# Delta-rule stage of a two-layer trunk: sums of squares in two single-pass products, and a new order on four engines

## The reference

```
def gated_delta_chunked(q, k, v, g, beta):   # q, k: unit norm per head
    G = jnp.cumsum(g, axis=-1)
    decay = jnp.where(incl, jnp.exp(jnp.where(incl, diff, 0.0)), 0.0)
    kk = jnp.einsum('bhnid,bhnjd->bhnij', k, k)
    lower = jnp.eye(CHUNK) + jnp.where(strict, beta * decay * kk, 0.0)
    sol = lax.linalg.triangular_solve(lower, rhs, ...)
    ...
    def step(S, inp):                         # over the chunks
        u = u_b - w_c @ S
        o = qd @ S + a_c @ u
        S = S * exp(gl) + kd.T @ u
...
q = l2_normalize(heads(qkv[..., :GDN_WIDTH]))          # x * rsqrt(sum(x*x) + EPS)
k = l2_normalize(heads(qkv[..., GDN_WIDTH:2 * GDN_WIDTH]))
```

## Time and profile before

| | |
|---|---|
| median of 3 runs | 3044.75 us (3042.94 to 3045.47) |
| the profiled execution | 3046.14 us, its span 3044.4 us |
| PE busy | 2972.9 us, 98% |
| DVE, ACT, POOL busy | 1531.4, 851.8, 426.4 us |
| mean granted TensorE clock | 0.99 of full speed |

### The profile page before, as it was taken

One profiled execution on the slowest core, in us unless ns is written; L12 is line 12 of the kernel. 1 busy time (PEld: TensorE's weight loads), 2 busy tenths in 40 slices (PEclk: granted clock), 3 DMA queues, 4 the chain that ended last, 5 costly groups with the idle time before them and its releaser, 6 DMA issues.

```text
span 3044.4 us, 47051 instructions
## 1 busy us (share of the span) xinstructions
PE 2972.9 (98%) x19124; PEld 2689.6 (88%) x19124; DVE 1531.4 (50%) x2163; ACT 851.8 (28%) x1521; POOL 426.4 (14%) x503
## 2 busy tenths in 40 slices
PE   8999989999999999999999999999999999999998
PEld 7999978887899999999999998788888888888887
DVE  5777447776443343444346443666743433333444
ACT  4211235555221111111113101566612111111112
POOL 2000145554120000000000000000021000100000
PEclk9999989999899999999999999999999999999999
DMA  3333321211111111111111425545211111111111
GB/s 121 92 92 98 107 72 52 63 63 57 33 57 49 41 48 48 41 41 48 49 48 38 151 86 165 140 99 118 59 49 56 41 55 48 48 44 46 48 41 70
DMA packets 201815, 207.31 MB, mean 68 GB/s; under 512 B 8363, under 2 KB 172348, under 8 KB 201676
## 3 DMA queue, kind: packets, MB, share of 16 engines
q1 hardware_dynamic: 191098, 167.05, 18.9%
q0 software_dynamic: 10368, 38.21, 3.7%
q10 hardware_dynamic: 210, 0.07, 0.0%
HBM read 162.87 MB, written 42.44 MB: 67 GB/s over the span
## 4 chain that ended last, share of the span: by engine, by line
PE 93%; DVE 2%; ACT 2%; issue 2%; POOL 1%; ACTq 0%; DVEq 0%; POOLq 0%
PE PS L1824 20%; PE PS L1823 20%; PE PS L1822 20%; PE PS L2237 5%; PE PS L2236 5%; PE PS L2235 5%; PE PS L2358 2%; PE PS L2342 2%; PE PS L2034 1%; PE PS L2309 1%; PE PS L2014 1%; PE PS L2308 1%; PE PS L1961 1%; DVE dec L1404 1%; PE PS L2051 1%
## 5 line engine op out<-in xcount | busy, mean ns | idle before, releaser
L1822 PE MATMUL PS<-YH,WL 128*128 128x348 f32 (+1 forms) x3040 | 1039.6, 342 | 4.4 <-DVE WL L1254 3.0
L1823 PE MATMUL PS<-YL,WH 128*128 128x348 f32 (+1 forms) x3040 | 1039.2, 342 | 0.0
L1824 PE MATMUL PS<-YH,WH 128*128 128x348 f32 (+1 forms) x3040 | 1038.4, 342 | 0.0
L1822 PEld LDWEIGHTS PS<-YH,WL 128*128 128x128 f32 x3040 | 572.0, 188 | 45.3 <-DVE WL L1254 3.3
L1823 PEld LDWEIGHTS PS<-YL,WH 128*128 128x128 f32 x3040 | 571.6, 188 | 37.9 <-issue 0.8
L1824 PEld LDWEIGHTS PS<-YH,WH 128*128 128x128 f32 x3040 | 573.0, 188 | 35.6
L1647 DVE TENSOR_TENSOR hT<-PS,hT 128x346 f32<-128x346 f32 (+2 forms) x440 | 251.3, 585 | 178.7 <-PE PS L2237 178.7
L2235 PE MATMUL PS<-AH,WL 128*128 128x346 f32 (+2 forms) x880 | 308.6, 351 | 1.1 <-DVE AL L1637 1.1
L2237 PE MATMUL PS<-AH,WH 128*128 128x346 f32 (+2 forms) x880 | 308.8, 351 | 0.0
L2236 PE MATMUL PS<-AL,WH 128*128 128x346 f32 (+2 forms) x880 | 308.8, 351 | 0.0
L794 POOL TENSOR_TENSOR gact<-gact,rs 128x346 f32<-128x346 f32 (+2 forms) x110 | 118.8, 1080 | 1307.0 <-ACT gact L1096 1307.0
(11 more groups left out here) (282 smaller groups left out, 3729.2 us busy)
## 6 DMA issues: line engine op xcount, KB each, us to landing
raw<-in_ffn_w_gate_up SPq DMA_DIRECT2D x88, 512.0 KB, 3.7
raw<-in_ffn_w_down SPq DMA_DIRECT2D x44, 512.0 KB, 3.6
s_in<-obuf POOLq DMA_DIRECT2D x32, 520.0 KB, 4.4
raw<-in_gdn_w_in SPq DMA_DIRECT2D x32, 512.0 KB, 4.2
Xqk<-s_in SPq DMA_DIRECT2D x10, 832.0 KB, 4.5
raw<-in_w_kv SPq DMA_DIRECT2D x16, 512.0 KB, 3.9
Xv<-s_in SPq DMA_DIRECT2D x10, 416.0 KB, 3.2
gBc<-s_g SPq DMA_DIRECT2D x10, 416.0 KB, 3.5
```

The lines of the kernel that those rows point to most:

```text
L1822: pe.matmul(PS[:, bank, 0:n], wl, xh, start=(k == 0), stop=False)
L1823: pe.matmul(PS[:, bank, 0:n], wh, xl, start=False, stop=False)
L1824: m = pe.matmul(PS[:, bank, 0:n], wh, xh, start=False, stop=(k == KT - 1))
```

## The change

`squares_high` on ACT squares keys and queries into a float32r tile `sqh` (one buffer for both g). POOL still makes the full squares, and `squares_low` on POOL subtracts the high part, giving `sql`. `key_sums` adds two float32r products, ones times high and ones times low, in place of each float32 product; chunk 0 keeps the old form. SP waits for `squares_high` of chunk c-2 ahead of the `Xqk` load. The loops of PE, ACT, DVE and POOL are written in a new order.

```
+            def squares_low(h, g):
+                pool.wait_ge(cs["sq"][g], h + 1)
+                pool.wait_ge(cs["shi"][g], h)
+                pool.tensor_tensor(sql[g][:, :, :], sq[g][:, :, :], sqh[:, :, :].bitcast(F32), ALU.subtract).then_inc(cs["slo"][g], 1)
...
+            def squares_high(h, g):
+                act.wait_ge(c_load, 16 * (h + 1))
+                if g:
+                    act.wait_ge(cs["kn"][0], h + 1)
+                else:
+                    act.wait_ge(cs["kn"][1], h)
+                src = Xqk[:, :, :].rearrange("p (w h) j -> p w h j", w=2)[:, :, HG * g:HG * g + HG, :]
+                act.activation(sqh[:, :, :].rearrange("p w (h j) -> p w h j", h=HG), src, ACT.Square).then_inc(cs["shi"][g], 1)
...
 (SP, ahead of the Xqk load of step c)
+                    if c > 1:
+                        sp.wait_ge(cs["shi"][g], c - 1)
...
 (PE, key_sums)
+                pe.wait_ge(cs["slo"][g], h)
+                for w in range(2):
+                    pe.matmul(PS[:, b0 + w, 0:GW], onesr[:, :], sqh[:, w, :], start=True, stop=False)
+                    m = pe.matmul(PS[:, b0 + w, 0:GW], onesr[:, :], sql[g][:, w, :], start=False, stop=True)
+                m.then_inc(cs["ss"][g], 1)
```

More of the change, by code:

```diff
@@ L743, in _ @@
                 tail, head = 0 <= t, h < NC
+                if tail:
+                    mask(t, 5, 0)
                 if levels:
-                    decayed(c, 1, 0)
+                    decayed(c, 0, 1)
                 if tail:
                     mask(t, 6, 0)
[L748 to L753, removed]
+                    mask(t, 6, 1)
                 if head and h:
@@ L756, in _ @@
                 if levels:
+                    first_mask(c, 0)
+                    decayed(c, 1, 0)
+                    first_mask(c, 1)
+                if head and h:
+                    squares_low(h, 0)
+                if levels:
                     mask(c, 1, 1)
+                    mask(c, 1, 0)
                     mask(c, 2, 1)
[L759 to L762, removed]
+                    mask(c, 2, 0)
                 if head and h:
                     squares(h, 1)
+                if levels:
+                    mask(c, 3, 1)
+                    decayed(c, 1, 1)
+                    mask(c, 4, 1)
+                    mask(c, 3, 0)
+                    mask(c, 4, 0)
+                    mask(c, 5, 1)
+                if tail and t < NC - 1:
+                    fade(t, 0)
+                if head:
+                    decayed(h, 0, 0)
+                if head and h:
+                    squares_low(h, 1)
                 if tail and t < NC - 1:
                     fade(t, 1)
[L767 to L776, removed]
             def accumulate(ph):
@@ L1001, in _ @@
                 if levels:
+                    values(c, 0)
+                if head and h:
+                    squares_high(h, 0)
+                if levels:
                     values(c, 1)
-                if head:
-                    decays(h, 1)
-                if levels:
+                    copy_x(c, 0, 1)
                     copy_x(c, 0, 0)
-                    copy_x(c, 0, 1)
-                    later_half(1, 1)
+                    later_half(c, 1, 1)
+                    later_half(c, 1, 0)
                 if head and h:
@@ L1011, in _ @@
                 if levels:
-                    later_half(1, 0)
+                    copy_x(c, 1, 1)
+                    later_half(c, 2, 0)
+                    copy_x(c, 1, 0)
+                if tail:
+                    result(t, 0)
+                if levels:
+                    later_half(c, 2, 1)
                 if head:
@@ L1015, in _ @@
                 if levels:
-                    copy_x(c, 1, 1)
-                    later_half(2, 1)
+                    copy_x(c, 2, 1)
+                if head and h:
+                    squares_high(h, 1)
+                if levels:
+                    later_half(c, 3, 1)
                 if tail:
                     result(t, 1)
[L1020 to L1023, removed]
                 if c == NC - 1:
@@ L1027, in _ @@
                 if levels:
[L1028 to L1033, removed]
+                    later_half(c, 3, 0)
+                    copy_x(c, 2, 0)
+                    copy_x(c, 3, 1)
                 if head and h:
@@ L1046, in _ @@
                     result_norm(t, 0)
+                if levels:
+                    copy_x(c, 4, 1)
+                    copy_x(c, 4, 0)
+                if tail:
+                    result_norm(t, 1)
                 if c == NC - 1:
@@ L1519, in _ @@
                     unit(h, 0)
[L1520 to L1524, removed]
                 if levels:
@@ L1534, in _ @@
                     low(0, 1)
+                if levels:
+                    add_u(c, 3, 1)
                 if head and h:
@@ L1537, in _ @@
                 if levels:
-                    add_u(c, 3, 1)
                     add_u(c, 3, 0)
-                if head:
-                    keys(h, 0)
+                if tail and t < NC - 1:
+                    state(t, 1)
+                    state(t, 0)
                 if tail:
-                    gated(t, 1)
+                    gated(t, 0)
                 if levels:
@@ L1565, in _ @@
                     first_m(h, 1)
-            gated(NC - 1, 0)
+                    keys(h, 1)
+                if tail:
+                    gated(t, 1)
+                if levels:
+                    updates(c, 1)
+                if c == NC:
+                    lo(2, P_GO.job0 + 3)
+                    lo(3, P_GO.job0 + 4)
             low(2, 0)
@@ L1953, in key_products @@
                     pe.wait_ge(cs["rn"][1], 1)
+                if h == 0 and g == 1:
+                    pe.wait_ge(taken, TAKEN0[P_GO])
                 if h > 1 and g == 0:
@@ L2107, in _ @@
                 tail, head = 0 <= t, h < NC
+                if levels:
+                    turned(c, 1)
                 if tail:
                     solved(t, 1)
+                if levels:
+                    level_x(c, 0, 1)
+                    level_x(c, 0, 0)
+                if tail:
                     solved(t, 0)
@@ L2118, in _ @@
                 if levels:
-                    level_u(c, 0, 0)
-                    level_u(c, 0, 1)
+                    level_x(c, 1, 1)
+                    level_x(c, 1, 0)
+                if tail:
+                    outputs(t, 0)
+                if levels:
+                    level_u(c, 1, 1)
                 if tail:
                     outputs(t, 1)
+                if c == NC:
+                    go_chunk(*GO_ORDER[1])
                 if levels:
-                    level_x(c, 1, 1)
+                    level_u(c, 1, 0)
+                    level_x(c, 2, 1)
                 if tail and t < NC - 1:
@@ L2127, in _ @@
                 if levels:
[L2128 to L2135, removed]
+                    level_u(c, 2, 1)
+                    level_x(c, 2, 0)
+                    level_x(c, 3, 1)
                 if tail and t < NC - 1:
@@ L2140, in _ @@
                 if levels:
[L2141 to L2146, removed]
+                    level_u(c, 2, 0)
+                    level_u(c, 3, 1)
+                    level_x(c, 3, 0)
                 if c == NC:
@@ L2166, in _ @@
                     level_x(c, 4, 0)
-                if head:
-                    turned(h, 1)
+                if tail:
+                    output_sums(t, 1)
+                if c == NC:
+                    go_chunk(*GO_ORDER[3])
                 if levels:
@@ L2172, in _ @@
                 if head:
+                    key_products(h, 0)
                     key_products(h, 1)
                 if levels:
+                    level_x(c, 5, 1)
                     level_x(c, 5, 0)
-                    level_x(c, 5, 1)
+                if head:
+                    turned(h, 0)
+                if levels:
+                    level_u(c, 5, 1)
+                    from_state(c, 1)
+                    level_u(c, 5, 0)
                 if head:
```

72 lines of the change are left out of this document (27 added, 45 removed).

## The result

| | before | after |
|---|---|---|
| median | 3045.11 us (4 runs, 3042.94 to 3046.45) | 3096.29 us (4 runs, 3092.26 to 3106.48) |
| ratio | | 1.017 (95% interval 1.0156 to 1.0184) |
| profiled execution | 3046.14 us | 3092.26 us |
| DVE, ACT, POOL busy | 1531.4, 851.8, 426.4 us | 1547.6, 868.4, 460.8 us |
| mean granted clock | 0.990 | 0.985 |

The change makes the kernel 51 us slower; 3076 was forecast, with a range up to 3092. The sign and the large step of the mechanism (a late load that PE waits for) came as predicted. A second wait came out more than twice as long as summed, and with it the size.

The account below looks back on a forecast made before the run. PE's own work was taken as the bound. Rounds 1 to 7 lose 4.5 us each (31.5), round 8 wins 1.3, early rounds add 1: 3046.1 becomes 3077.3, median 3076; own range 3060 to 3092, 8-in-10 range 3033 to 3092.

Parts of the forecast that it names:

- The sign: Whole kernel: slower than before, 3076 us forecast; slower had a chance of 0.71, faster 0.20.
- large step: Ahead of `first_t(h, 0)`: PE idles 2.65 us a round, as POOL's `first_mask` stands behind `squares` and the late `Xqk` load.
- A second wait: PE at `level_x(c, 3, 0)`: waits for `add_u(c, 2, 0)`, held behind `differences(h, 0)` on DVE; 0.9 us a round.
- The second wait: PE behind `first_t(h, 0)`: waits another 0.7 us a round while POOL does `decayed` and `first_mask(h, 1)`.
- the small one: PE at `level_x(c, 3, 0)`: waits 0.9 us, bounds 0 to 1.5, for `add_u(c, 2, 0)` behind the moved `differences(h, 0)`.
- round 8: Round 8 of the delta stage: no further load, so it wins 1.3 us.
- The 2.5 us taken for a round: Behind the gaps at `first_t`: the clock falls each round, costing 1.6 to 3.4 us, taken as 2.5.
- the round of 36.5 us at full clock: Delta-stage round: 33.56 - 1.28 + 0.9 + 2.65 + 0.7 = 36.5 us, 2.0 more than before.
- The clock stays up: Rival: the gap ahead of `first_t` comes but the clock does not fall; 3059 us, chance 0.15.
- The new order holds: Rival: PE remains bound by its work and both gaps at `first_t` vanish; 3033 or 3025 us, chance 0.20.
- About even: Rival: landing after 4.6 us and `differences` in its short form, a round of 34.4; 3045 us, chance 0.08.
- Float32r no cheaper: Rival: float32r passes of `key_sums` cost as much as float32, 12 us more on top; 3088 us, chance 0.02.

Follow-up runs that it names:

- e7: Changed kernel plus three useless float32 products on PE ahead of the wait of `first_t(h, 0)` in rounds 1 to 7; 3097.17 us, ratio 1.0166.
- e3: Changed kernel, but SP issues the `Xqk` load ahead of the `gBc` load; 3062.78 us, ratio 1.0060 to the kernel before.
- e4: Changed kernel, but POOL does both `first_mask` and `decayed(c, 1, 0)` ahead of `squares(h, 0)`; 3070.53 us, ratio 1.0078 to the kernel before.
- e8: Changed kernel with `decays(h, 1)` on ACT moved to directly behind `norms(h, 1)`; 3064.28 us, ratio 1.0065 to the kernel before.
- e5: Changed kernel with `differences(h, 0)` on DVE moved behind `add_u(c, 3, 0)`; 3073.23 us, ratio 1.0092 to the kernel before.
- e2: Changed kernel with the float32 `key_sums`, without `squares_high`, `squares_low` and SP's wait (new order alone); 3076.96 us, ratio 1.0100 to the kernel before.
- e10: Changed kernel with `differences(h, 0)` later on DVE and three useless products ahead of `first_t(h, 0)` in rounds 1 to 7; 3067.13 us, ratio 1.0073.
- e9: Changed kernel with `Xqk` load first and `differences(h, 0)` later, but the old float32 products, without `squares_high` and `squares_low`; 3040.24 us, ratio 0.9986.
- e6: Changed kernel with both repairs, `Xqk` load ahead of `gBc` and `differences(h, 0)` behind `add_u(c, 3, 0)`; 3035.34 us, ratio 0.9964 to the kernel before.
- e1: Kernel before, in its old order, with only the new float32r products added; 3049.14 us, ratio 1.0013.

## Why the prediction was wrong, and where it was right

**The large step was right**, and its size too. From PE's start behind `output_sums(t, 1)` (689.83) to `first_t(h, 0)` (701.39) pass 11.56 us; 11.5 was summed. The gap was 2.06 to 2.99 us in rounds 1 to 7, 2.6 on average (2.65), the landing 5.8 us (5.8), `squares_low` 1.95 (2.05). The second wait, for `first_mask(h, 1)`, was 0.70 as computed where the clock was up (e7), and hidden where it was low. e3, e4 and e8 each take the gap away by a different link of the chain, which shows the chain.

**The step that failed is the small one: `level_x(c, 3, 0)`.** I bounded that wait by 0 and 1.5 us, the 1.5 from no row, and took 0.9, the size it had in its old place. It was 2.13 to 2.15 in every one of the eight steady rounds, 1.25 over the term, and e5, which takes it away, runs 23 us faster. The fault lies in taking L1404's 3.65 us as the long form although I had just put the longer `squares_low` beside it: each of the four instructions waits for about one POOL item, so 1.96 + 1.06 + 0.7 + 1.07 gives 4.8, against 4.83 measured. With 3.65 us the same chain would leave about 2.15 - 1.18 = 0.97 us, by my estimate, so the 0.9 was right for the length that it was read at. e2 (no `squares_low`: 2.19 us, no gap) and e5 show that cause. I had the mechanism in the lock that the Trainium skill describes (SBUF — State Buffer, "SBUF: two separate sides"), and the trace agrees with it (0.95 us alone, 4.83 beside POOL); I did not carry the new item's length through it.

**What hung on it.** First, a gap of 2.15 us is itself large enough to lower the clock, and the sum had one fall in a round. The trace after has falls behind both gaps, the second kind in four of eight rounds (at 520, 643, 684 and 766 us); one such fall costs 1.5 us in e3. Second, round 8, which I had winning 1.3 us because it has no late load, also has this gap with its fall, and it begins in the low stretch that round 7's late mask leaves behind: 38.90 us, 4.4 lost.

**Clock.** The 2.5 us taken for a round was too much, and a mistake on the other side hid part of that. A fall behind `first_t` costs about 0.9 net (e10), not 1.6 to 3.4; I had not asked who sets the pace just after the gap. The falls at the second gap, which I did not have, add 1.5 in about every second round, so that the two kinds together come to some 1.6 a round (an estimate from e3 and e10).

**Not seen at all:** `gated(t, 1)` at the round's end also runs beside `squares_low` and the masks (its two instructions take 1.94 and 1.84 us at 664.99, against 0.58 and 0.65 for `gated(t, 0)`) and delays `add_u`, so `level_x(c, 1, 1)` waits 0.34 to 0.87 us in five of the rounds 1 to 7 (0.46 on average); and PE's bare work in the new order is 34.0 us (e9) against 33.56 before, a term of 0.45, spread in pieces of some 0.1 us over many groups, for which I have no cause. `key_sums` went to 0.83, not 0.76. With these, the round of 36.5 us at full clock becomes 36.5 + 1.25 + 0.46 + 0.45 + 0.14 + 1.6 = 40.4, against 40.7 measured. My range had no place for this: the terms named with it, the dearest clock and 5 us for the ends, add up to 3087 and not to its 3092, and none stands for a second fall in a round.

Together, for the profiled execution: rounds 1 to 7 took 40.7 on average, 6.2 over 34.49, 43.5 us in all (31.5 forecast); round 8 +4.4 (-1.3); the rounds ahead +4.4, of them 2.1 until the first `first_t` (+1); the end from `first_t` of the last chunk to the output projection 42.8 against 48.5 us, -5.7 (0). The same stretch takes 43.9 to 44.2 us in e2, e3, e6 and e9 and 47.5 in e1, so its gain belongs to the new order; the mean granted clock in it is 0.75 before and 0.88 after, and no run tests more than that. The four parts add up to 46.6 us, against 46.1 measured. The median lies 4 us above that execution: the four runs span 14 us, and the longer the run, the lower its mean clock (0.985 at 3092.26, 0.983 at 3094.55, 0.982 at 3098.03, 0.979 at 3106.48). That fits a number of falls that differs from run to run; it was not tested by itself. Before, with gaps of 0.93 us, four runs span 3.5 us and the thirteen timed beside e1 6.2.

**The rivals.** "The clock stays up" (3059) fell by the windows. "The new order holds" (3033) describes the repaired kernel (3035), not this one; what separated the two were the late load and the late differences. "About even" (3045) fell by both of its conditions: the landing took 5.8 us and `differences` 4.83. "Float32r no cheaper" fell: 0.83 against 1.40.

## What to carry to other kernels

Where an order is written out by hand, follow each load back through the DMA queue to the last instruction it waits for, and price it issued as it will be, behind its neighbour: one `decays` moved by a third of a round turned a load with time to spare into a gap in every round. And when work is added to GpSimd, give every VectorE instruction beside it that reads two operands from SBUF the new item's length, not the length it showed before. Near 98% of TensorE, two such repairs (one DMA earlier, one DVE item later) were worth 61 us, and the cheaper products 5 to 7.

## What the runs showed of the hardware that was not expected

- Gaps of like length do not always lower the granted clock. In the changed kernel it fell behind the gap at `first_t` (2.06 to 2.99 us) in every one of rounds 1 to 7, but behind the 2.13 to 2.15 us at `level_x(c, 3, 0)` in four of eight; in e3 seven of eight steady rounds fell behind 2.14 us, and the one from 639.09 to 674.44 did not. A gap of 1.64 us in round 0 of the changed kernel (at 456.47) was followed by a fall, one of 1.54 at the same place in e5 was not. Most low stretches in the steady rounds lasted 3.4 us, a few 6.8.
- A fall of the clock costs less where another engine sets the pace behind it: 1.5 us in e3 (36.88 against 35.35), some 0.9 net behind `first_t` (e5 against e10, 3073.23 to 3067.13), where PE waits for POOL as soon as it is faster.
- Keeping the clock up at one gap can move the fall to another: in e7 the falls behind `first_t` went, those behind `level_x(c, 3, 0)` rose from four rounds of eight to eight, and the time stayed (3096.29 and 3097.17).
